# mLSTM stage of a two-layer hybrid trunk: the scratch rows that are broadcast to 128 partitions, stored so that a broadcast reads one run of 4 KB instead of four of 1 KB

## What is computed

```python
# prompt: chunks of tokens, in order; c (128 x 128) and n per head
def step(carry, inp):
    c, n, m = carry
    qc, kc, vc, ic, fc = inp
    bcum = jnp.cumsum(fc, axis=-1)
    log_intra = where(causal, bcum[..., :, None] - bcum[..., None, :] + ic[..., None, :], -inf)
    log_inter = bcum + m[..., None]
    m_t = maximum(log_inter, max(log_intra, axis=-1))
    w_intra = exp(log_intra - m_t[..., None])
    w_inter = exp(log_inter - m_t)
    s = einsum('bhtk,bhsk->bhts', qc, kc) * w_intra
    num = einsum('bhts,bhsv->bhtv', s, vc) + w_inter[..., None] * einsum('bhvk,bhtk->bhtv', c, qc)
    ...
    c_new = w_old[..., None, None] * c + einsum('bhs,bhsv,bhsk->bhvk', w_tok, vc, kc)
```

## Time and profile before

| what | us |
|---|---|
| median of three runs | 2996.88 |
| profiled execution, its own time | 3008.62 |
| its span, first to last instruction | 3006.8 |
| PE busy | 2778.9 (92%) |
| DVE / ACT / POOL busy | 992.9 / 595.1 / 786.9 |
| DMA in the chain that ended last | 5% of the span |
| landing of a decay load (512 KB, 8 of them), median | 8.9 |
| landing of a key and query load (512 KB, 8 of them), median | 8.6 |
| landing of a weight panel (512 KB, in_w_up, 64 of them), median | 4.1 |

### The profile page before, as it was taken

One profiled execution on the slowest core, in us unless ns is written; L12 is line 12 of the kernel. 1 busy time (PEld: TensorE's weight loads), 2 busy tenths in 40 slices (PEclk: granted clock), 3 DMA queues, 4 the chain that ended last, 5 costly groups with the idle time before them and its releaser, 6 DMA issues.

```text
span 3006.8 us, 40907 instructions
## 1 busy us (share of the span) xinstructions
PE 2778.9 (92%) x16185; PEld 2393.5 (80%) x16185; DVE 992.9 (33%) x1947; ACT 595.1 (20%) x1267; POOL 786.9 (26%) x432
## 2 busy tenths in 40 slices
PE   7999646999999999999699999888599999999999
PEld 4666444699999999999455655566499999999999
DVE  4111343342222222254242233444445222222224
ACT  2000342111100111120232232333212100011103
POOL 2300121143433334323000000122344434334331
PEclk9999878999999999999798998998799999999999
DMA  3111341021111111110100000465211111111111
GB/s 98 41 37 35 79 90 50 28 78 50 42 49 49 42 49 43 41 49 25 53 18 18 14 4 0 150 216 182 67 55 50 43 49 47 44 49 44 47 35 56
DMA packets 192198, 166.41 MB, mean 55 GB/s; under 512 B 15956, under 2 KB 183158, under 8 KB 187805
## 3 DMA queue, kind: packets, MB, share of 16 engines
q1 hardware_dynamic: 181765, 121.62, 14.2%
q0 software_dynamic: 7584, 41.98, 4.1%
q10 hardware_dynamic: 2752, 1.47, 0.2%
HBM read 155.88 MB, written 9.37 MB: 55 GB/s over the span
## 4 chain that ended last, share of the span: by engine, by line
PE 85%; DVE 5%; DMA 5%; issue 2%; ACT 1%; POOL 1%; SPq 0%; ACTq 0%; DVEq 0%; POOLq 0%
PE psum L1754 24%; PE psum L1770 23%; PE psum L481 18%; PE psum L1796 5%; PE psum L1889 3%; PE psum L1888 2%; PE psum L1945 2%; PE psum L1908 2%; DMA M<-in_cache_rope_k,idx 1%; DMA Z<-in_cache_rope_k,idx 1%; PE psum L1898 1%; DMA G<-decay_scratch 1%; PE psum L1957 1%; PE psum L1980 0%; DVE Zr L427 0%
## 5 line engine op out<-in xcount | busy, mean ns | idle before, releaser
L1754 PE MATMUL psum<-Gr,Mr 128*128 128x344 f32 x1536 | 367.7, 321 | 0.0
L1770 PE MATMUL psum<-Zr 128*128 128x344 f32 x2304 | 365.9, 320 | 1.2 <-DVE x L1365 1.2
L1770 PE MATMUL psum<-Zr,Mr 128*128 128x344 f32 x2304 | 365.7, 320 | 0.0
L1754 PE MATMUL psum<-Gr,Zr 128*128 128x344 f32 x1536 | 365.4, 320 | 0.0
L1770 PEld LDWEIGHTS psum<-Zr 128*128 128x128 f32 x2304 | 363.4, 188 | 1.5 <-DVE x L1365 1.5
L1770 PEld LDWEIGHTS psum<-Zr,Mr 128*128 128x128 f32 x2304 | 363.5, 188 | 0.0
L1365 DVE TENSOR_TENSOR x<-psum,x 128x344 f32<-128x344 f32 x384 | 197.6, 515 | 472.7 <-PE psum L1770 472.7
L929 ACT ACTIVATE Zr<-M 128x344 fp32r<-128x344 f32 x192 | 94.5, 492 | 1181.7 <-DVE M L1353 1181.7
L481 PE MATMUL psum<-G,W 128*128 128x344 f32 (+1 forms) x1008 | 297.2, 458 | 8.6 <-DVE G L362 6.5
L736 POOL TENSOR_TENSOR Zr<-W,ones 128x1024 fp32r<-128x1024 f32 x75 | 145.7, 1943 | 549.8 <-PE psum L1770 232.9
L736 POOL TENSOR_TENSOR Mr<-W,ones 128x1024 fp32r<-128x1024 f32 x68 | 131.6, 1936 | 573.8 <-PE psum L1754 216.4
(11 more groups left out here) (321 smaller groups left out, 3157.4 us busy)
## 6 DMA issues: line engine op xcount, KB each, us to landing
W<-in_w_up SPq DMA_DIRECT2D x64, 512.0 KB, 4.1
W<-in_w_down SPq DMA_DIRECT2D x64, 512.0 KB, 3.4
W<-in_w_in SPq DMA_DIRECT2D x26, 512.0 KB, 3.9
W<-in_w_out SPq DMA_DIRECT2D x16, 512.0 KB, 4.0
Z<-in_x_prompt SPq DMA_DIRECT2D x8, 512.0 KB, 6.8
G<-decay_scratch SPq DMA_DIRECT2D x8, 512.0 KB, 8.9
M<-kq_scratch SPq DMA_DIRECT2D x8, 512.0 KB, 8.6
out_y_p<-Z SPq DMA_DIRECT2D x8, 512.0 KB
```

The source lines that it names most:

```text
L1754: mm = pe.matmul(bank[v % DBANKS][:, 0:TB], w[:, k, :], r[:, k, blk(b)], start=(k == 0 and c == 0), stop=(k == KD - 1 and c == 2))
L1770: mm = pe.matmul(bank[v % DBANKS][:, 0:TB], w[:, k, :], r[:, k, blk(b)], start=(k == 0 and c == 0), stop=(k == KH - 1 and c == 2))
```

## The change

The scratch tensors are stored chunk-major and sample-major, so that the four heads' 1 KB stand next to each other, and the third decay, which nobody reads from memory, is no longer stored. A broadcast then reads one run of 4 KB for each partition, where it read four runs of 1 KB, 12 KB apart (decays: 8 rows of 1536 bytes) or 8 KB apart (keys and queries: 8 rows of 1 KB). The writing side is split by head: four DMAs instead of one for the decays, four instead of two for keys and queries. So that a head's key and query can leave in one run, DVE stages the key first and the query second, and the two readers of `srow` swap their index. Two wait values follow the number of stores.

```diff
-        rows_d = nc.dram_tensor("decay_scratch", (HC, 3 * CH), F32).ap()
+        rows_d = nc.dram_tensor("decay_scratch", (NC, H, 2 * CH), F32).ap()
-        kq_d = nc.dram_tensor("kq_scratch", (HC, 2 * P), F32).ap()
+        kq_d = nc.dram_tensor("kq_scratch", (NS, H, 2 * P), F32).ap()
...
-        rows_v = rows_d.rearrange("(h c) n -> c h n", h=H)
-        kq_v = kq_d.rearrange("(h b) n -> b h n", h=H)
+        rows_v = rows_d.rearrange("c h n -> c (h n)")
+        kq_v = kq_d.rearrange("b h n -> b (h n)")
...
-                sp.dma_start(bc[s].rearrange("p h a t -> p h (a t)"),
-                             rows_v[ds(n, 1), :, 0:2 * CH].to_broadcast([P, H, 2 * CH])).then_inc(sem(f"bc_in{s}"), 16)
+                sp.dma_start(bc[s].rearrange("p h a t -> p (h a t)"),
+                             rows_v[ds(n, 1), :].to_broadcast([P, H * 2 * CH])).then_inc(sem(f"bc_in{s}"), 16)
...
-                sp.dma_start(kqb[s].rearrange("p h a d -> p h (a d)"),
-                             kq_v[ds(n, 1), :, :].to_broadcast([P, H, 2 * P])).then_inc(sem(f"cs_in{s}"), 16)
+                sp.dma_start(kqb[s].rearrange("p h a d -> p (h a d)"),
+                             kq_v[ds(n, 1), :].to_broadcast([P, H * 2 * P])).then_inc(sem(f"cs_in{s}"), 16)
...
-            sp.wait_ge(sem("scratch_out"), 32)
+            sp.wait_ge(sem("scratch_out"), 16 + 16 * H)
...
-            sp.wait_ge(sem("kq_out"), 32)
+            sp.wait_ge(sem("kq_out"), 16 * H)
...
-            act.dma_start(rows_d, rows3.rearrange("r a t -> r (a t)")).then_inc(sem("scratch_out"), 16)
+            for h in range(H):
+                act.dma_start(rows_d[:, h, :], rows3[h * NC:(h + 1) * NC, 0:2, :].rearrange("r a t -> r (a t)"))\
+                   .then_inc(sem("scratch_out"), 16)
...
-            for j, r in ((0, 1), (1, 0)):
-                act.dma_start(kq_d.rearrange("r (a d) -> r a d", a=2)[:, j, :], srow[:, r, :]).then_inc(sem("kq_out"), 16)
+            for h in range(H):
+                act.dma_start(kq_d[:, h, :], srow[h * NS:(h + 1) * NS, 0:2, :].rearrange("r a d -> r (a d)"))\
+                   .then_inc(sem("kq_out"), 16)
...
-            for j, (k0, s_) in enumerate(((0, 1.0), (4, K_SCALE), (8, 1.0))):
+            for j, (k0, s_) in enumerate(((4, K_SCALE), (0, 1.0), (8, 1.0))):
```

More of the change, by code:

```diff
@@ L1191, in _ @@
             step(dve.tensor_scalar(snn, sn, scol[:, 5:6], None, ALU.mult))
-            dve.scalar_tensor_tensor(out=snn, in0=srow[:, 1, :], scalar=scol[:, 6:7], in1=snn, op0=ALU.mult, op1=ALU.add)\
+            dve.scalar_tensor_tensor(out=snn, in0=srow[:, 0, :], scalar=scol[:, 6:7], in1=snn, op0=ALU.mult, op1=ALU.add)\
                .then_inc(sem("s_nnew"), 1)
             dve.wait_ge(sem("s_nnew"), 1)
-            step(dve.tensor_tensor(sjunk, snn, srow[:, 0, :], ALU.mult))
+            step(dve.tensor_tensor(sjunk, snn, srow[:, 1, :], ALU.mult))
             step(dve.tensor_reduce(scol[:, 8:9], sjunk, AX.X, ALU.add))
```

## The result

The changed kernel took 2963.47 us (median of 4 runs, 2960.83 to 2966.81) against 2995.57 for the kernel before (4 runs, 2991.86 to 3010.27). The ratio is not the quotient of the two medians: 0.9884 of 2995.57 would be 35 us less, with 24 to 45 as its interval.

The account below looks back on a forecast made before the run. Five decay landings in the ring of waits were taken to bound the changed stage. Landings of 24.8 us instead of 46.2 take 21.4 off the profiled 3008.62, giving 2987.2; the median stands 11.7 lower: 2975.5 us, range 2968 to 2998.

Parts of the forecast that it names:

- The ring: Per chunk: decay landing, POOL's instructions, SP's state store, next loads, next decay landing; turns of 17.1 us, half of it landing.
- flat 90 GB/s: Last key and query load: after the state load's peak, a stretch at 89 to 92 GB/s, forecast to reach 250 or more.
- run and place don't matter: Rival, chance 0.11: loads are slow because 128 partitions read the same bytes, wherever these stand; no change, 2997 us.
- a concentrated run is slower: Rival, chance 0.09: all sixteen DMA engines meet at one place in the 4 KB run; 19 us more, 3016 us.
- only the decays' own distance is matched: Rival, chance 0.08: a 4 KB run serves 173 GB/s and no more; 8 us less, 2989 us.
- early takeover by another wait: Rival, chance 0.04: DVE's tail and POOL's instructions collide, turns keep at 15 us; five times 2 us less, 2987 us.
- address below 8 KB: Broadcast reads meet at a memory place set by that address: 8 KB apart one place, 12 KB two, adjacent 4 KB four.
- The landing: Decay load, issue to landing: 1.5 us plus 3.45 us for 1.05 MB at 304 GB/s, 4.95 us for each of five.
- The turn: POOL's first instruction from chunk to chunk, chunks 3 to 7: 17.1 less 4.3, so 12.8 us, still ended by decays.
- The sum of 21.4 us: Stage's gain: five decay landings of chunks 3 to 7 take 24.8 us instead of 46.2; other parts counted as nothing.
- The part ahead of chunk 2: POOL's earlier start on chunks 0 and 1 meets DVE's small steps, stretched by 1 us each; 0, 1 us either way.
- nothing behind it changes length: Sign of being right: the stage ends 21 us earlier and all parts of the program after it keep their length.

Follow-up runs that it names:

- early: The change, with SP issuing the decays of chunk n+3 ahead of the store of sample n; 2956.07 us against 2984.63 for the kernel before, ratio 0.9893.
- kq12k: The kernel before with key and query rows of 1.5 KB, so both loads' runs stand 12 KB apart; 2982.87 us against 2990.0, ratio 0.9974.
- pad9k: The kernel before with 128 bytes behind each row of both scratch tensors, runs 9 KB apart; 2965.15 us against 2984.63, ratio 0.9931.
- decay_only: The kernel before with only the decays stored by chunk, keys and queries still 8 KB apart; 2985.34 us against 2988.04, ratio 0.9989.
- gap4k: The change with a gap behind each head, so four 1 KB runs stand 4 KB apart; 2972.51 us against 2990.0 for the kernel before, ratio 0.9939.
- near4: The change with 256 bytes behind each head, so four 1 KB runs stand 1.25 KB apart; 2968.65 us against 2988.04 for the kernel before, ratio 0.9925.
- decay8k: The kernel before with decay rows of 1 KB, so the decays too stand 8 KB apart; 2995.94 us against 2988.04, ratio 1.003.

## Why the prediction was right and wrong

**The path: right.** The ring was the path. Five decay landings set the turns before and after, and once they were taken off it ("early") turns fell to what DVE sets.

**Which load is slow, and why: mostly right.** The flat 90 GB/s of the key and query load went, and moving this load alone brought 2.7 of the 3.3 us per turn. The rival that run and place don't matter fell (kq12k, pad9k), and so did the one that a concentrated run is slower. The rival that only the decays' own distance is matched fell with decay_only and with the 260 to 456 GB/s of a 4 KB run, and the early takeover by another wait fell because the decays still end POOL's wait in turns of 13.8 us. Wrong is the place as "address below 8 KB": by it gap4k and kq12k had to be equal, and gap4k should have been clearly slower than the change; turns are 14.1, 15.9 and 13.8, though the last key and query load takes the same time in the first two (5.2 and 5.1 us). Which addresses meet stays open, and so does whether they meet in memory at all: the runs vary distances and show rates, not the place of the wait. Runs show 8 KB slow, 12 KB between, and 1, 1.25, 2, 9 KB fast and 4 KB nearly so in the turn.

**The landing: right, a little short.** Forecast 4.95 us, measured 5.5 and 5.3 in the median. The turn was forecast at 12.8 us and came to 13.8 and 13.4. The 12.8 has a slip of its own: it takes off a fifth of 21.4 us, in which the 10.74 us of chunk 3 count, but the four turns hold only the landings of chunks 4 to 7. Those average 8.9 us, so 4.95 us each leaves a turn of 13.2. The rest, 0.6 and 0.2 us, is mostly the landing, and in the first profile one late issue: the key and query load took 1.17 us to issue once, else 0.46, where it had been 0.37. (The 38.9 us of the page's estimate and of the concentrated rival should be 38.7, which changes nothing.) The sum of 21.4 us for the stage stands against 22.9 in the first pair of profiles, and against 20.3 as the mean of two profiles of each kernel (163.0 and 142.7). Of the 20.3, 19.2 lie between POOL's chunks 2 and 7, where the five landings are.

**What I costed at nothing.** ACT's added stores and the swap on DVE are no piece of the chain of waits. The part ahead of chunk 2 was given 1 us either way, for DVE's stretched steps. From the end of the input projection to POOL's chunk 2 it took 38.0 and 36.5 us before and 35.5 and 37.1 after, but 40.5 in near4 and 39.6 in pad9k. The stretched steps are not the reason: from DVE's first small step to PE's first product of the loop it is 10.8 us before, 10.8 after and 10.9 in near4, with four steps stretched in each. Two other things vary, the landing of the pooling weights that DVE's chain waits for, and TensorE's clock in chunk 1. In the profile of the change:

```profile
332.23 3.21 DMA M<-in_pool_w
...
353.44 1.16 PE psum L1649 x8
```

and in near4, for the same two:

```profile
332.48 5.32 DMA M<-in_pool_w
...
355.86 2.08 PE psum L1650 x8
```

Together they give 2.5 us either way where I had allowed 1, and with them come the 147 us stages of kernels whose turns equal the change's. The same stretch takes 39.7 us in decay_only, which has neither gap nor padding, and 35.5 in decay8k, which speaks for scatter; those kernels' profiles were not repeated. The last key and query load gave nothing in the change, as said: from POOL's chunk 7 to the output projection 39.5 and 38.1 us before, 37.8 and 39.6 after.

**The step that failed** is the last one of the sum, from the profiled execution to the median: "nothing behind it changes length", and the line that "the runs' own spread puts 4 us on either end". Both put the 2500 us behind the stage at nearly nothing. In the first pair of profiles that part differs by 22.7 us, as much as the stage itself, and over fourteen profiles it runs over 26 us, from 2487.6 to 2513.6, with no order by kernel. The three runs of the kernel before, on which the range rested, already lay 16 us apart, and their median of 2996.88 compares with 2984.63, 2988.04 and 2990.0 over 13 to 23 later runs.

What the whole gained is known less well than the stage. In the first comparison the medians are 2995.57 and 2963.47, in the second, with 23 and 6 runs, 2990.0 and 2967.64. The second pair is 22.4 us apart, 1 us from the forecast; of the 9.7 us between the two differences 5.6 lie in the kernel before and 4.2 in the change. I put them down to the scatter, but that is argued and not shown: the chip may have changed too, and the ratio of the second comparison (0.9908) allows 20 to 35 us. The longer executions are those with the lower clock: of the 23 runs before, the three fastest (2980.06 to 2980.78 us) have a mean granted clock of 0.961 to 0.962, the three slowest (2999.93 to 3000.26 us) 0.953 to 0.955. What gives an execution the one or the other stays open. That 22.4 comes so close to 21.4 is in part luck.

## What to carry to other kernels

When many partitions load the same few rows, look at the rate of one such load with nothing behind it: a flat stretch far below the rate of a plain load, with the DMA engines mostly idle, points to where the rows lie. Try another row pitch first; here 128 bytes of padding gave the same turn as the new layout. And look at what the slow load stands ahead of on its queue: here nobody waited for it in the ring, and moving it alone took 2.7 us from each turn. If a landing is part of a ring, issuing it one step earlier takes it off: with the old layout that alone shortened the stage by 29 us, the new layout alone by 20. By the medians of the whole program the two are equal (21.4 and 22.4 us), so the order of the two is shown for the stage only.

## What the runs showed of the hardware that I had not expected

Four runs of 1 KB, each read by all 128 partitions, come at 90 GB/s when they stand 8 KB apart and at 312 to 379 GB/s when they stand 1.25 KB apart, with the same number and size of runs. In the turn, 9 KB is as good as one run, and 12 KB is worse than 4. And one program's part of 2500 us that nothing changed varied by 26 us (1%) between executions, so a change of 0.7% needs its own stretch of the profile to be sized: 6 runs against 23 still left the ratio open by 0.25% either way.
